# Cached values of a paged decode moved two turns nearer to their keys: which turn of a hand-written schedule issues which matmul

## The reference, cut to what is computed

```python
def fox_decode(q, k, v, logf, k_past, v_past, logf_past):
    suffix = (lax.cumsum(lfp, axis=1, reverse=True) - lfp).transpose(0, 2, 1)
    cq = jnp.cumsum(logf, axis=1).transpose(0, 2, 1)
    s_past = einsum('bqhd,bkhd->bhqk', qf, k_past) + cq[..., None] + suffix[:, :, None, :]
    s_new = einsum('bqhd,bkhd->bhqk', qf, k) + cq[..., :, None] - cq[..., None, :]
    s_new = jnp.where(causal, s_new, NEG)
    p = jax.nn.softmax(jnp.concatenate([s_past, s_new], axis=-1), axis=-1)
    return einsum('bhqk,bkhd->bqhd', p[..., :p_len], v_past) + einsum(..., p[..., p_len:], v)
```

## Time and profile before

| | us |
|---|---|
| median of 3 runs | 1293.64 (1292.74 to 1295.45) |
| the profiled execution, its time | 1294.23 |
| the profiled execution, its span in the trace | 1292.3 |
| PE busy in the span | 1261.5 (98%) |
| ACT busy, DVE busy | 474.8, 589.4 |
| mean granted TensorE clock | 0.994 of full speed |

### The profile page before, as it was taken

The page is one execution under the profiler, slowest core; times in us unless marked ns, Lnnn a source line. Parts: engine busy times, 40 slices in busy tenths (PEclk is TensorE's granted clock), DMA queues, the critical chain, the costliest instruction groups (busy, mean ns, idle before and its releaser), DMA issues.

```text
span 1292.3 us, 29960 instructions
## 1 busy us (share of the span) xinstructions
PE 1261.5 (98%) x12437; PEld 1180.6 (91%) x12437; DVE 589.4 (46%) x1096; ACT 474.8 (37%) x765; POOL 110.4 (9%) x247
## 2 busy tenths in 40 slices
PE   9999999999999999998898999999999999999997
PEld 8999999999999999996555666699999999999997
DVE  6644332244354433236765676645443521343433
ACT  6543221122233112434867777543222310222222
POOL 1000000000013000000223522122000000000000
PEclk9999999999999999999989999999999999999999
DMA  8323422232322352355699999333323322323301
GB/s 202 98 82 81 144 85 65 65 95 67 122 90 66 117 144 65 115 177 163 239 370 324 342 343 360 133 99 84 98 79 114 103 77 65 96 66 105 112 11 70
DMA packets 186649, 172.35 MB, mean 133 GB/s; under 512 B 11393, under 2 KB 149154, under 8 KB 186562
## 3 DMA queue, kind: packets, MB, share of 16 engines
q1 hardware_dynamic: 185394, 167.47, 41.2%
q0 software_dynamic: 1104, 3.67, 0.8%
q10 hardware_dynamic: 64, 0.02, 0.0%
HBM read 162.19 MB, written 8.93 MB: 132 GB/s over the span
## 4 chain that ended last, share of the span: by engine, by line
PE 91%; DVE 4%; issue 2%; ACT 2%; DMA 1%; SPq 0%; ACTq 0%; DVEq 0%
PE ps L2156 78%; PE ps L989 2%; PE ps L1074 2%; PE ps L1089 2%; PE ps L914 1%; DMA d_keys<-in_cache_k 1%; PE ps L954 1%; PE ps L934 1%; ACT d_keysT L1334 1%; PE ps L752 0%; PE ps L2296 0%; DMA gain_rows<-in_norm_final 0%; PE ps L895 0%; PE ps L2310 0%; DVE ps L1791 0%
## 5 line engine op out<-in xcount | busy, mean ns | idle before, releaser
L2156 PE MATMUL ps<-n_hi,w_hi 128*128 128x272 f32 x1856 | 387.1, 288 | 2.0 <-DVE w_lo L2626 0.8
L2156 PE MATMUL ps<-n_hi,w_lo 128*128 128x272 f32 x1856 | 386.8, 288 | 0.0
L2156 PE MATMUL ps<-n_lo,w_hi 128*128 128x272 f32 x1856 | 385.2, 288 | 0.0
L2346 ACT ACTIVATE w_hi<-w_raw 128x2048 fp32r<-128x2048 f32 (+2 forms) x76 | 156.0, 2052 | 540.7 <-PE ps L2156 540.6
L2156 PEld LDWEIGHTS ps<-n_hi,w_hi 128*128 128x128 f32 x1856 | 292.9, 188 | 2.7 <-issue 2.5
L2156 PEld LDWEIGHTS ps<-n_lo,w_hi 128*128 128x128 f32 x1856 | 292.7, 189 | 0.0
L2156 PEld LDWEIGHTS ps<-n_hi,w_lo 128*128 128x128 f32 x1856 | 290.7, 189 | 0.0
L2500 DVE TENSOR_TENSOR w_lo<-w_raw,w_hi 128x2048 fp32r<-128x2048 f32 (+2 forms) x75 | 191.6, 2555 | 49.5 <-ACT w_hi L2346 49.5
L2156 PE MATMUL ps<-g_hi,w_lo 128*128 128x272 f32 x704 | 145.7, 288 | 0.0
L2156 PE MATMUL ps<-g_hi,w_hi 128*128 128x272 f32 x704 | 145.5, 288 | 0.0
L2156 PE MATMUL ps<-g_lo,w_hi 128*128 128x272 f32 x704 | 145.2, 288 | 0.0
(11 more groups left out here) (360 smaller groups left out, 1230.4 us busy)
## 6 DMA issues: line engine op xcount, KB each, us to landing
w_raw<-in_ffn_w_in SPq DMA_DIRECT2D x87, 512.0 KB, 4.9
d_keys<-in_cache_k SPq DMA_DIRECT2D x128, 256.0 KB, 5.3
d_values<-in_cache_v SPq DMA_DIRECT2D x124, 256.0 KB, 6.1
w_raw<-in_w_in_mix SPq DMA_DIRECT2D x28, 512.0 KB, 4.7
w_raw<-in_ffn_w_out SPq DMA_DIRECT2D x16, 768.0 KB, 5.5
w_raw<-in_ffn_w_out SPq DMA_DIRECT2D x16, 640.0 KB, 4.8
w_raw<-in_w_out_mix SPq DMA_DIRECT2D x8, 512.0 KB, 4.9
suffix_scratch<-d_log_f_sums SPq DMA_DIRECT2D x32, 64.0 KB, 2.1
```

The costliest lines, as they stand in the source:

```text
L2156: mm = pe.matmul(bank(4 * j + 2 * t + half), wp, xp[:, k, half * HALF:(half + 1) * HALF], start=(k == 0 and wp is w[0] and xp is x_hi), st ...
L2346: nc.scalar.activation(w_hi[j][:, 0:kt * UC], w_raw[j][:, 0:kt * UC], ACT.Copy).then_inc(w_hi_ready, 1)
```

## The change

The pairs of cached values are taken two turns sooner: half 0 in turns 8b+7 to 8b+10, half 1 in 8b+11 to 8b+14. In the last batch half 0 is in turns 63 to 66, one pair to a turn, and half 1 stays in turns 67 and 68. For this the transposes of half 0 and their copies go from i = 7 to i = 6. The new tokens' values stay with k = 3 of half 0, but for batch 0, where they stay in turn 12 (now k = 1 of half 1). In a turn that has a pair with k = 0, `values` now follows both calls of `scores`. The copies of the output and the turning of it move with the values (`COPY_AT`, `OUT_AT`: 8b+22 becomes 8b+19), and the correction (L1834, L1398) goes from i = 4 to i = 3. No instruction and no transfer is added or removed.

```diff
--- before.py
+++ after.py
@@ -368,8 +368,8 @@
         def value_turn(b, half, k):
 
             if b == DB - 1:
-                return 8 * b + (9 if half == 0 else 11) + k // 2
-            return 8 * b + (9 if half == 0 else 13) + k
+                return 8 * b + (7 + k if half == 0 else 11 + k // 2)
+            return 8 * b + (7 if half == 0 else 11) + k
 
         VALUE_PAIRS = sorted(((b, half, k) for b in range(DB) for half in range(2) for k in range(4)),
                              key=lambda v: (value_turn(*v), v))
@@ -392,9 +392,12 @@
             r = RING_PAIRS.index(w)
             return d_v[r % V_RING], dv_landed[r % V_RING], 32 * (r // V_RING + 1)
 
+        NEW_AT = [(0, 1, 1)] + [(b, 0, 3) for b in range(1, DB)]
+
         def values_through(b, half):
 
-            return 2 * VALUE_PAIRS.index((b, half, 3)) + 2
+            last = NEW_AT[b] if half == 0 else (b, 1, 3)
+            return 2 * VALUE_PAIRS.index(last) + 2
 
         def keys_copied(x):
 
@@ -1015,7 +1018,7 @@
                     mm = pe.matmul(ps[0:NR, B_M, M_NEW:M_NEW + NS], d_q[b % 2][:, j * NR:(j + 1) * NR],
                                    pT[:, T_FK + j, SEQ:T], start=(j == 0), stop=(j == NJ - 1), skip_group_check=True)
                 mm.then_inc(new_done, 1)
-            if i == 7 and b < DB:
+            if i == 6 and b < DB:
                 pe.wait_ge(dexp[0], 2 * b + 2)
                 if b == 1:
                     pe.wait_ge(pt_copied[1], 1)
@@ -1059,7 +1062,7 @@
                                            stop=True, skip_group_check=True)
                     mm.then_inc(oT_done, 1)
 
-        OUT_AT = [8 * b + 22 for b in range(DB - 2)] + [67, 70]
+        OUT_AT = [8 * b + 19 for b in range(DB - 1)] + [70]
 
         def products_tensor(pe, x):
 
@@ -1100,7 +1103,7 @@
                 pe.matmul(ps[:, B_O, :], d_pTn[b % 2][:, :], d_vn[:, :], start=False, stop=False, skip_group_check=True)
 
             for w, (b, half, k) in values_of(x):
-                if half == 0 and k == 3:
+                if (b, half, k) == NEW_AT[b]:
                     new_values(b)
             y = x - 1
             active = 0 <= y < 2 * DB * SETS
@@ -1115,10 +1118,16 @@
                 if i % 4 == 0 and b:
                     pe.wait_ge(dexp[i // 4], 2 * b if i == 0 else b)
                 scores(y, 0)
-            for w, (b, half, k) in values_of(x):
-                values(w, b, half, k)
+            due = values_of(x)
+            late = any(k == 0 for _, (b, half, k) in due)
+            if not late:
+                for w, (b, half, k) in due:
+                    values(w, b, half, k)
             if active:
                 scores(y, 1)
+            if late:
+                for w, (b, half, k) in due:
+                    values(w, b, half, k)
 
         def mix_tensor(pe, gated_product):
             pe.wait_ge(drained, 2 * P_MIX_OUT)
@@ -1387,17 +1396,17 @@
                 for half in range(2):
                     if x == COPY_AT[c][half]:
                         copy_out(c, half)
-            if i == 7 and b < DB:
+            if i == 6 and b < DB:
                 copy_probsT(b, 0)
             if i == 2 and 1 <= b <= DB:
                 copy_probsT(b - 1, 1)
             if i == 3 and b + 1 < DB:
                 query(b + 1)
-            if i == 4 and 1 <= b <= DB:
+            if i == 3 and 1 <= b <= DB:
                 act.wait_ge(dd_step, b)
                 nc.scalar.activation(d_sm[:, 3:4], d_sm[:, 2:3], ACT.Exp, scale=-1.0).then_inc(de_done, 1)
 
-        COPY_AT = [(8 * b + 15, 8 * b + 17) for b in range(DB - 1)] + [(67, 69)]
+        COPY_AT = [(8 * b + 13, 8 * b + 16) for b in range(DB - 1)] + [(68, 69)]
 
         def forget_scalar(act, x):
             if x == 0:
```

## The result

| | before | after |
|---|---|---|
| median, us (4 runs each, same chip) | 1294.53 (1292.74 to 1295.45) | 1304.98 (1303.77 to 1305.44) |
| ratio, 95% interval | | 1.0084 (1.0069 to 1.0099) |
| the profiled execution, its time and span | 1294.23, 1292.3 | 1305.44, 1303.4 |
| turn 0 starts | 589.49 | 589.33 |
| turn 20 starts | 655.82 | 657.22 |

The change costs 10.5 us. In the profiled executions it is 11.1 us of span: +1.56 up to turn 20, +10.98 from turn 20 to turn 63, -1.3 behind it. PE's lines in the mix stage have numbers higher by 3 in the new kernel (L1089 is now L1092), ACT's and DVE's by 9 (L1334 is L1343).

A forecast was written before the change was run, and what follows sets the result against it. PE's instruction list was taken as the bound, with the cached-page stream near its limit in places. 18.3 - 0.76 - 0.60 + 0.9 - 0.7, less 0.7, gave +16.4 us: 1310.6, median 1310.0; forecast 1306 to 1315, range 1300 to 1318.

The forecast's parts named there:

- Collisions, their number and price: Mix stage, batches 0 to 6: 28 turns where value pairs meet scores on the same column groups, 0.87 us each.
- The seven ahead of turn 20: Colliding turns 7, 8, 11, 12, 15, 16, 19: covered by PE's gaps and low clock, counted as nothing (0 to +2).
- The other 21: Colliding turns from 20 to 60: 21 x 0.87 = 18.3 us, with only the gaps of turns 31 and 42 covering.
- rival 3: Behind turn 20 all 9 us of PE's gaps close and 3 us of half-speed stretches go: 1300; chance 0.15.
- They shift with PE and cover nothing: Gaps ahead of turns 23 and 27 (1.19, 1.82 us) end a chain starting with PE's own work, so cover nothing.
- The late pair of turn 31: PE's gap ahead of a value matmul in turn 31, taken for a late page, would be covered: -0.76 us.
- The key page of turn 42: PE's wait for a key page before turn 42 hangs on transfers and would be covered: -0.60 us.
- Transposes of half 0: Turn 8b+6: PE waits for ACT's exponential behind the keys' transposes, mainly in batch 3: +0.9 us (0 to +2).
- Output steps sooner: Turn 8b+19: turning the output sooner puts DVE's picks out of the transposes' way by three turns: nothing.
- Page stream the bound: Mix stage: the stream of pages hides all collisions and the head start gains 2.7 us: median 1291.0; chance 0.08.
- Strict order: PE takes matmuls strictly in order, so collisions cost nothing and only side terms are left: 1292 to 1294; chance 0.04.
- Nothing covered: All 28 collisions are paid in full, 28 x 0.87 + 0.9 = 25.3 us: 1319; chance 0.10.

The follow-up runs named there:

- the kernel without collisions: Changed kernel, value pairs with k = 0 and 1 writing the other two column groups, decode output not the reference's: 1294.18 us, ratio 0.9987 to the kernel before.
- the two other kernels with 28 collisions: Changed kernel with the halves' output groups swapped: 1304.14 us, ratio 1.0074; changed kernel with k = 0 pairs between the scores again: 1304.64 us, ratio 1.0075.
- the one with the shifted list: Kernel before with 64 long-fulfilled waits put into PE's list at turn 18, nothing else: 1295.72 us, ratio 1.0008.
- the 56 collisions: Kernel before with the two halves' output column groups swapped and no step moved, so all 56 pairs meet scores on their groups: 1319.62 us, ratio 1.0204.
- the run with the output sooner: Kernel before with only the turning of the output three turns sooner (8b+19 instead of 8b+22): 1297.44 us, ratio 1.0023.

## Why the prediction was right, point by point

It said slower, 1310, 1300 to 1318; measured 1304.98. Direction, mechanism and range held. The middle was 5 us too high.

**Collisions, their number and price: right.** 28 turns, at 8b+7, 8b+8, 8b+11, 8b+12, as counted from the groups in the code. 0.86 us against the predicted 0.87, which was read from lone pairs. Against the kernel without collisions, idle time and low clock taken off, 25 of the 28 turns are longer by 0.76 to 0.92 us; turns 7, 16 and 56 by 0.3 to 0.4.

**The seven ahead of turn 20, counted at nothing (0 to +2): right.** Turn 20 starts 1.56 us later, counted from turn 0, at 657.22, just past the "655 to 657". The key pages are no longer waited for ahead of turns 18 and 20 (1.87 and 1.22 before): this cover is used up.

**The other 21, 18.3 us with 2 us off: here the size was wrong.** Predicted +17 from turn 20 to turn 63, measured +10.98. The step that failed is the choice to list just two gaps as cover, and nothing for the clock. From turn 20 on PE's idle time falls from 8.18 to 4.70 us, though waits of 1.31 (turn 22, in the place of 1.19 ahead of turn 23), 0.97 (turn 30) and 0.78 (in turn 27, for DVE's `h_k` behind the moved picks) came in. The stops in turns 31 and 33 (0.76, 0.86), the wait for ACT's `h_k_nat` in turn 42 (0.83) and most of those for DVE's `o_nat` in turns 49 and 56 (0.93 and 0.45, 0.26 left) are gone.

The clock gave 1.7: the rows show a granted clock below 1 in turns 18, 23, 24 and 27 before (of the two levels, 1.2 GHz for part of each), after in 2, 3, 14, 15, 22 and 23; summed over turns 20 to 62 that costs 3.4 us before and 1.7 after, over turns 0 to 19 it is 1.7 and 3.4. Where these stretches fall isn't a matter of the change: the traces of the two other kernels with 28 collisions show none in turns 0 to 62.

So 21 x 0.86 = 18.1, less 3.5 and 1.7, leaves 12.9 for the measured 11.0. Of the 2 us between, 0.6 is what the stop in turn 31 cost beyond the 0.76 us shown (last section), and 1.0 that the 21 turns are longer by 17.1 us against the kernel without collisions, and not by 18.1. So rival 3, "more is covered", holds half: it closed all 9 us of gaps and 3 us of clock, and measured are 3.5 and 1.7.

"They shift with PE and cover nothing", said of the waits ahead of turns 23 and 27, was right for the collisions: the kernel without any has the same 1.31 us in turn 22 and 0.61 ahead of turn 27. What took the latter from 1.82 to 0.78 are two moved steps, for which the prediction's sum has no term. In the kernel before ACT copies the output between the exponential and the keys' copies that PE waits for; in the new one it does so a turn sooner, and the exponential stands 3.26 us ahead of turn 27 instead of 3.87. And the new tokens' values now take 0.43 us of PE in turn 26. The two make up 1.04; this is read from the rows, no run moves them alone. The copy in the kernel before, the new tokens' values in the changed one, and the wait in the one without collisions:

```profile
678.58 0.59 ACT L1377 ACTIVATE d_out<-ps 64x512 f32<-64x512 f32 x1
```

```profile
681.02 0.50 PE L1103 MATMUL ps<-d_new_values,d_probT_new 96*128 96x512 f32 x1
```

```profile
679.80 0.71 PE L992 MATMUL ps<-ident,d_keys 64*128 64x64 f32 x16 [0.61 <-ACT d_keysT L1345]
```

A collision does cover such a wait where it stands behind the start of the chain: with the groups swapped turns 25 and 26 collide, on either kernel, and no wait is left ahead of turn 27. My reading: the collision lengthens PE's turn while ACT's copy and DVE's maxima go on.

Against the kernel without collisions the same sum runs over turns 0 to 63: 28 x 0.86 = 24.1, less idle time (19.9 us there, 9.7 in the changed kernel) 10.2, clock equal, gives 13.9; its turn 63 starts 10.2 us sooner, counted from turn 0. The turns with collisions account for 21.8 us and not 24.1, and the other turns are 1.4 us shorter in the changed kernel, which no run explains. Of the 6.6 us of idle time that closes behind turn 20, 4.55 are four stops for blocks of the list; this one trace has them, so here the cover is partly luck.

Where every pair collides, no gap at all is left behind turn 20 and 4.3 us in turns 0 to 62 (18.7 before), and a collision still has a net price of 0.47. There the 54 collisions up to turn 63 account for 42.2 us, 0.78 each; less 14.4 of idle time and 3.4 of clock that is the measured 24.3. So with a longer turn the waits for ACT, for a page and for the list's next block all shrink, and the net price is what this leaves.

**The late pair of turn 31, -0.76: the right amount for the wrong reason.** I took the gap for a late page. It stands inside a pair, behind a block of instructions, and vanished with its place in the list. The run without collisions and the one with the shifted list show none in turn 31 either.

**The key page of turn 42, -0.60: for the most part wrong.** 0.42 us of waiting is left there, now for DVE's copy of the keys.

**Transposes of half 0, +0.9: right.** In turns 6, 14, 22 and 30 PE's idle time changes by -0.60, +0.17, +0.11 and +0.98, +0.7 in all. Of the +3.4 us of its run 3.0 belong to `OUT_AT`.

**Output steps sooner, "Nothing": wrong as a step by itself.** It cost 3.0 us on the kernel before. DVE's picks weren't out of the way but ahead of `h_k`, which brought a wait of 0.64 us in turn 27; a wait of 0.76 for ACT came in turn 44; and stops for the list's next block stand in turns 52 and 54. What each is worth in the medians stays open. The changed kernel has the wait in turn 27 (0.78), 0.17 in turn 44 and no gap in turns 52 and 54, so the step's price there is inside the -1.7 us (up to +0.4) of everything but the collisions.

**The end, -0.7: direction right.** -1.3 behind turn 63, of which the correction alone gave 0.9. The rest is less than the up to 1 us by which this stretch differs between kernels with the same end.

**SP and the transfers, nothing: right.** DMA share falls as predicted, from 0.98 to 0.90, and the run without collisions, with the same loads, loses nothing.

**The rivals.** Page stream the bound (0.08): refuted by the 56 collisions, which move no load and cost 26.4 us. Strict order (0.04): refuted by the same pair of timelines. The Trainium skill, page "TensorE: Matmul & The Clock Gate", section "Part 3: Packing small matmuls — row/col tiling", has matmuls start and end strictly in program order, by which both should look alike; the measurement decides against it for instructions on different column groups. Nothing covered (0.10): refuted, half is.

## What to carry to other kernels

When matmuls of a quarter of the array run beside each other, the output partition of each is part of the schedule: write down the column groups that meet in every turn before moving one, since a clash costs its whole length on the engine and none of it shows as a wait. Then expect to pay about half of it in a kernel that has idle slivers in every turn, as here with 0.41 to 0.47 of 0.86 us over 14, 28 and 56 clashes. Test a bundle of small side steps one by one, as the waits that the trace shows need not be what costs.

## What was not expected of the hardware

PE waits for its own instructions. With the DMA engines near full (share 1.05, 388 GB/s from 760 to 765 us in the run with the output sooner), it stood 0.5 to 2.35 us until 1.21 to 1.52 us behind the end of a 16 KB packet of instructions, 31 times in fourteen traces. In the 3 us ahead of each of these 31 packets the share was 0.90 to 1.06. Which instruction that hits hangs on how many come before it: 64 idle waits in turn 18 took it away from turn 31 and put another into turn 50. Such a stop inside turn 31 made the turn 1.39 us longer (4.43 against 3.04 with the list shifted) for 0.76 us of shown idle time; my reading is that matmuls around the stop which run without their neighbours count as busy. With longer PE turns the stops were rarer: the three kernels with 28 collisions have one, one and two of over 0.5 us, the one with 56 none, the one without collisions four.
